# A streaming encoder layer on eight cores: norm row spread by TensorE, last block in halves, order replanned

## The reference

```python
u = rmsnorm(x, norm_mix)
xl, gl, xp, gp, ml, mp = jnp.split(u @ w_in, SPLITS, axis=-1)     # 5632 columns
xc = causal_conv(xl)                                              # depthwise, width 4
r, i = sigmoid(block_diag(xc, w_rg_a) + b_a), sigmoid(block_diag(xc, w_rg_i) + b_i)
a = exp(-8 * r * softplus(-lam))
h = scan(h = a * h + sqrt(1 - a * a) * i * xc)                    # along the frames
A = h * silu(gl)
B = (pooled_means_minus_frame(xp) @ w_pool + b_pool) * pool_scale * silu(gp)
x = x + (sigmoid(ml) * A + sigmoid(mp) * B) @ w_out
x = x + sigmoid(rmsnorm(x, norm_ple) @ w_ple_gate) * (p @ w_ple)
y = rmsnorm(x, final_norm)
```

## Time and profile before

| what | value |
|---|---|
| median of 3 runs (lowest, highest) | 1022.29 us (1022.08, 1022.36) |
| the profiled execution | 1022.78 us |
| its span (slowest core, core 2) | 1020.9 us |
| spans of cores 0 to 7 | 1018.6, 1009.3, 1020.9, 1011.4, 1018.9, 1009.3, 1009.8, 1016.7 us |
| busy: PE, DVE, ACT, POOL | 941.1, 782.4, 758.2, 310.7 us |
| DMA | 184.14 MB, 180 GB/s in the mean |

### The profile page before, as it was taken

One profiled execution on the slowest core, in us unless ns is written; L12 is line 12 of the kernel. 1 busy time (PEld: TensorE's weight loads), 2 busy tenths in 40 slices (PEclk: granted clock), 3 DMA queues, 4 the chain that ended last, 5 costly groups with the idle time before them and its releaser, 6 DMA issues.

```text
span 1020.9 us, 16786 instructions; the slowest of 8 cores (1009.3 to 1020.9 us)
## 1 busy us (share of the span) xinstructions
PE 941.1 (92%) x4545; PEld 435.1 (43%) x4636; DVE 782.4 (77%) x1208; ACT 758.2 (74%) x1275; POOL 310.7 (30%) x576
## 2 busy tenths in 40 slices
PE   3897998499999999999999999999999999999994
PEld 1342443144444444444444444444444445454541
DVE  3755978667697696686969788787969797798864
ACT  3777786766857858769696867778796959999753
POOL 3332424223143142312313123333414243232221
PEclk9998999799999999999999999999999999999998
DMA  8899775898943667466664667465773647467732
GB/s 186 166 251 228 162 169 101 238 229 212 252 117 113 191 200 228 129 198 178 181 188 124 233 164 200 137 199 170 223 200 105 190 135 221 151 188 242 233 99 83
DMA packets 113179, 184.14 MB, mean 180 GB/s; under 512 B 67392, under 2 KB 72000, under 8 KB 113088
## 3 DMA queue, kind: packets, MB, share of 16 engines
q1 hardware_dynamic: 100272, 154.69, 50.8%
q0 software_dynamic: 12816, 28.38, 14.5%
HBM read 155.56 MB, written 29.12 MB: 181 GB/s over the span
## 4 chain that ended last, share of the span: by engine, by line
PE 62%; ACT 14%; issue 9%; DMA 9%; DVE 5%; POOL 0%; ACTq 0%; SPq 0%; DVEq 0%; POOLq 0%
PE psum L814 42%; PE psum L1121 8%; PE psum L1101 8%; DMA wpg<-w_in 4%; PE psum L1128 2%; ACT wk L927 1%; DMA ring<-w_in 1%; ACT L927 1%; DVE wk L868 1%; PE psum L886 1%; DMA xb<-xp 1%; ACT L909 1%; ACT wk L925 1%; ACT u2t L1113 1%; PE psum L889 1%
## 5 line engine op out<-in xcount | busy, mean ns | idle before, releaser
L814 PE MATMUL psum<-ut,ring 128*128 128x512 bf16 x2444 | 555.5, 379 | 9.4 <-ACT wk L1048 2.7
L814 PEld LDWEIGHTS psum<-ut,ring 128*128 128x128 bf16 x2496 | 241.9, 98 | 298.0 <-issue 13.7
L868 DVE SCALAR_TENSOR_TENSOR wk<-xw,cvec,wk 128x512 f32<-128x512 f32 x186 | 133.3, 744 | 15.5 <-ACT wk L859 4.0
L732 POOL TENSOR_SCALAR stat<-stat 128x1 f32<-128x1 f32 x99 | 39.8, 402 | 278.3 <-ACT wk L1140 134.1
L1121 PE MATMUL psum<-wpg,u2t 128*128 128x512 bf16 x517 | 119.1, 379 | 2.0 <-DMA u2t<-ub 1.3
L1101 PE MATMUL psum<-wout,mg 128*128 128x512 bf16 x499 | 116.0, 379 | 2.8 <-ACT ws L1048 0.9
L814 PE MATMUL psum<-ut,wpg 128*128 128x512 bf16 x312 | 77.5, 401 | 21.2 <-ACT wk L1050 12.0
L1121 PEld LDWEIGHTS psum<-wpg,u2t 128*128 128x128 bf16 x528 | 51.4, 98 | 64.1 <-issue 3.1
L1101 PEld LDWEIGHTS psum<-wout,mg 128*128 128x128 bf16 x512 | 49.7, 98 | 61.8 <-issue 3.0
L948 POOL COPY hst<-wk 128x1 f32<-128x1 f32 x43 | 51.6, 1212 | 70.9 <-DVE wk L943 67.0
L879 ACT ACTIVATE xcb<-wk 128x512 bf16<-128x512 f32 x62 | 39.1, 630 | 44.7 <-DVE wk L868 44.3
(11 more groups left out here) (189 smaller groups left out, 1480.4 us busy)
## 6 DMA issues: line engine op xcount, KB each, us to landing
ring<-win_bf SPq DMA_DIRECT2D x154, 512.0 KB, 4.6
xb<-xp SPq DMA_DIRECT2D x64, 512.0 KB, 6.1
yp<-xb SPq DMA_DIRECT2D x32, 512.0 KB, 3.3
ring<-w_in POOLq DMA_DIRECT2D x12, 512.0 KB, 8.2
win_bf<-ring POOLq DMA_DIRECT2D x12, 512.0 KB, 15.7
wpg<-w_in POOLq DMA_DIRECT2D x10, 512.0 KB, 9.1
win_bf<-wpg POOLq DMA_DIRECT2D x10, 512.0 KB, 11.6
xb<-w_ple_gate SPq DMA_DIRECT2D x8, 512.0 KB, 5.5
```

The costliest lines, as they stand in the source:

```text
L814: nd("pe", pe_cost(8, N), [lambda e, kc=kc: e.matmul(b.ap[:, 0:N], lhsT=s.ap.rearrange("p (k n) -> p k n", k=8)[:, kc, o:o + 128], rhs=ut_ ...
L868: nd("dve", dve_cost(N), lambda e, j=j, w=w: e.scalar_tensor_tensor(out=av(), in0=xw()[:, :, 3 - j:W - j], scalar=w, in1=av(), op0=ALU.mul ...
```

## The change

- norm_mix is no longer read spread over 128 partitions by one DMA on SP. Two DMAs of 2 KB on ACT's queue bring it as rows of one partition, two float32 matmuls with a row of ones times 32 spread them into PSUM, and DVE copies them to `gmbc`.
- The small vectors (`cvec`) are loaded first on ACT's queue; what is derived from them (`consts` before, with an Exp and an Ln on ACT) comes at the very start.
- pool_scale and final_norm come from the host spread over 128 rows, so that their loads are plain ones.
- The sums of squares of tiles 0 and 1 write their unused output to a work tile, not to `ub`. Weight block 0 waits for x block 2.
- The slots `xb` are tracked in two halves. In the very last prompt block the squares, the last product and the store go by halves of 512 columns (L1275, L1284, L1287 of the new kernel), with one more POOL addition (L1278). The last block of tile 7 and that of tile 8 are turned by TensorE (L1239) and copied from PSUM (L1242 on ACT or L1244 on DVE).
- Every node has a tag of kind, tile and part, and a table `ORDER` adds a shift to its due time; POOL's computing steps have none. Some of the planner's numbers are others.

The core of the diff; of the table and the tags a line or two stand for all:

```diff
 D = 1024
 IN_COLS = 5632
 NPAIR = IN_COLS // 256
-PRM = dict(window=61003.0, lim=113076.0, lag=10051.0, penw=1.36, slack=78.0, evac=255.0, p2=0, c2=0.55, 
-           a2=0.94, an=0.2, cs=12784.0, wl=30305.0, pes=12.0, late=(), wq='pool', wd=6037.0, pet=2, 
...
-           nu=3, nx=3, ac=3)
+           nr=5, nu=3, nx=3, ac=3)
+
+ORDER = {"a0.0": 1759, "a0.1": 11360, "a0.2": 14842, "a0.3": 16186, "a1.0": -5600, "a1.1": -27034, "a1.2": 21723,
...
-        n.eng, n.cost, n.nom, n.tset = eng, cost, nom, tset
+        n.eng, n.cost, n.tset = eng, cost, tset
         if eng != "pe" and any((r[0] if isinstance(r, tuple) else r).pool == "fb" for r in reads):
-            n.nom = nom = nom - PRM["evac"]
+            nom = nom - PRM["evac"]
+        n.tag = self.tag if eng != "pool" or queue is not None else ""
+        n.nom = nom = nom + ORDER.get(n.tag, 0.0)
...
-                d0 = max(s + 900.0, dma_free)
+                d0 = max(s + 1000.0, dma_free)
                 dma_free = d0 + n.nbytes
-                end = dma_free + 1300.0 + PRM["dl"]
+                end = dma_free + 1700.0
                 lat = 60.0
...
-    d_pool_scale = din("pool_scale", [1024])
+    d_pool_scale = din("pool_scale", [128, 1024])
-    d_final_norm = din("final_norm", [1024])
+    d_final_norm = din("final_norm", [128, 1024])
...
-    mkpool("xb", 6, [128, 1024], F32)
+    mkpool("xb", 6, [128, 1024], F32, nsub=2)
...
+    def xb2(v):
+        return [(v, 0), (v, 1)]
+
...
-        return nd(queue, 560.0 if queue == "pool" else SPC,
+        return nd(queue, {"pool": 560.0, "act": 100.0}.get(queue, SPC),
-                  reads=list(reads), writes=[dst], nom=nom, nbytes=nbytes, queue=queue, soft=soft, nb=nb, gates=gates,
+                  reads=list(reads), writes=xb2(dst) if isinstance(dst, V) and dst.pool == "xb" else [dst],
...
+    load(CV, d_vecs, -99000, 200, queue="act")
+    Z.tag = "cv"
+    nd("dve", 100, lambda e: e.tensor_scalar(out=CV2.ap[:, HBA:HBA + 16], in0=CV.ap[:, BA:BA + 16], scalar1=0.5,
+                                             scalar2=None, op0=ALU.mult), reads=[CV], writes=[CV2], nom=-97000)
...
+    nd("act", 250, lambda e: e.activation(out=CV2.ap[:, HCL:HCL + 8], in_=CV.ap[:, LAM:LAM + 8], func=AF.Exp,
+                                          scale=-1.0), reads=[CV], writes=[CV2], nom=-97000, tset=(LN, EXP))
+    nd("act", 250, lambda e: e.activation(out=CV2.ap[:, HCL:HCL + 8], in_=CV2.ap[:, HCL:HCL + 8], func=AF.Ln, bias=1.0),
+       reads=[CV2], writes=[CV2], nom=-97000, tset=(LN,))
...
+    ones = Z.val("ws")
+    nd("pool", 100, lambda e: e.memset(ones.ap[0:1, :], 32.0), writes=[ones], nom=-99000)
+    for hf in range(2):
+        row, bank = Z.val("wk"), Z.val("fb")
+        nd("act", 100, lambda e, row=row, hf=hf: e.dma_start(out=row.ap[0:1, :], in_=d_norm_mix[hf * 512:(hf + 1) * 512].unsqueeze(0)),
+           writes=[row], nom=-98000, nbytes=30, queue="act")
+        nd("pe", 1800, lambda e, row=row, bank=bank: e.matmul(bank.ap, lhsT=ones.ap[0:1, :], rhs=row.ap[0:1, :],
+                                                              start=True, stop=True),
+           reads=[ones, row], writes=[bank], nom=-96000)
+        nd("dve", dve_cost(512), lambda e, bank=bank, hf=hf: e.tensor_copy(
+            out=GM.ap[:, hf * 512:(hf + 1) * 512], in_=bank.ap), reads=[bank], writes=[GM], nom=-95000)
+
...
-        n = load(dst, x_src(tiles[j // 4], j % 4), -90000 + 2000 * j if j < 4 else -22000 + 1000 * j, 1750, gates=gates)
+        n = load(dst, x_src(tiles[j // 4], j % 4), -90000 + 2000 * j if j < 4 else -22000 + 1000 * j, 1600, gates=gates)
         x_first.append(n)
-        if j == 0:
-            load(GM, d_norm_mix.partition_broadcast(128), -89000, 1750)
-            nd("dve", 650, lambda e: e.tensor_scalar(out=GM.ap, in0=GM.ap, scalar1=32.0, scalar2=None, op0=ALU.mult),
-               reads=[GM], writes=[GM], nom=-89000)
-        if j == 3:
-            load(CV, d_vecs, -83500, 300)
-
-    load(G3, d_final_norm.partition_broadcast(128), 150000, 1750, nb=150000)
+
+    load(G3, d_final_norm, 150000, 1650, nb=150000)
...
+            junk = Z.val("wk") if S["idx"] < 2 else u
             nd("act", act_cost(1024, False, acc=True),
-               lambda e, x=x, st=st, u=u: e.activation(out=u.ap, in_=x.ap, func=AF.Square, accum_out=st.ap[:, 0:1]),
-               reads=[x], writes=[st, u], nom=nom)
+               lambda e, x=x, st=st, junk=junk: e.activation(
+                   out=junk.ap if junk.pool == "ub" else junk.ap.bitcast(BF16), in_=x.ap, func=AF.Square,
+                   accum_out=st.ap[:, 0:1]),
+               reads=xb2(x), writes=[st, junk], nom=nom)
             rstd_ops(st, nom)
...
-                turn(u, lambda j=j: ut_v()[:, :, j * 128:(j + 1) * 128], (UT, j), nom, 1800)
+                turn(u, lambda j=j: ut_v()[:, :, j * 128:(j + 1) * 128], (UT, j), nom, 1300)
...
-                    gates = [x_first[2 * k + 1 if k < 2 else 5] if k in (0, 1, 3) else w_first[k - 1 if k < 4 else k - 2]]
-                n = load(s, d_w_in[m], -25000.0 + 2000 * k if gates and k < 4 else nom - PRM["wl"], 3000, queue="pool", gates=gates)
+                    gates = [x_first[(2, 3, 0, 5)[k]] if k in (0, 1, 3) else w_first[k - 1 if k < 4 else k - 2]]
+                n = load(s, d_w_in[m], -25000.0 + 2000 * k if gates and k < 4 else nom - PRM["wl"], 3200, queue="pool", gates=gates)
...
-                load(s, d_wsc[m], nom - PRM["wl"], 1750, reads=[WSC[m]], soft=PRM["sl"])
+                load(s, d_wsc[m], nom - PRM["wl"], 1650, reads=[WSC[m]], soft=PRM["sl"])
...
-                   reads=[s], writes=[WSC[m]], nom=nom + PRM["wd"], nbytes=1750, queue=PRM["wq"], soft=PRM["sw"], paced=True,
+                   reads=[s], writes=[WSC[m]], nom=nom + PRM["wd"], nbytes=2050, queue=PRM["wq"], soft=PRM["sw"], paced=True,
...
+                    op=ALU.add), reads=[(xr, hf), d[hf]], writes=[(xr, hf)], nom=nom)
             nd("act", act_cost(1024, False), lambda e, xr=xr, u2=u2: e.activation(out=u2.ap, in_=xr.ap, func=AF.Copy),
-               reads=[xr], writes=[u2], nom=nom,
...
-                out=u2t.ap, in_=xr.ap, func=AF.Square, accum_out=st.ap[:, 0:1]), reads=[xr], writes=[st, u2t], nom=nom)
+                out=u2t.ap, in_=xr.ap, func=AF.Square, accum_out=st.ap[:, 0:1]), reads=xb2(xr), writes=[st, u2t], nom=nom)
             rstd_ops(st, nom)
-            turn(u2, lambda u2t=u2t: u2t.ap.rearrange("p (k n) -> p k n", k=8), u2t, nom, 1800)
+            end_ = S["idx"] == 7 and j == 3
+            if S["idx"] >= 7 and j >= nt - 1:
+                tb = Z.val("fb")
+                nd("pe", pe_cost(8, 128), [lambda e, u2=u2, tb=tb, c=c: e.transpose(
+                    out=tb.ap.bitcast(BF16)[:, c * 128:(c + 1) * 128], in_=u2.ap[:, c * 128:(c + 1) * 128],
+                    identity=IDB.ap) for c in range(8)], reads=[u2, IDB], writes=[tb], nom=nom)
+                nd("act", act_cost(1024), lambda e, tb=tb, u2t=u2t: e.activation(
+                    out=u2t.ap, in_=tb.ap.bitcast(BF16), func=AF.Copy), reads=[tb], writes=[u2t], nom=nom,
+                   alt=("dve", dve_cost(1024), lambda e, tb=tb, u2t=u2t: e.tensor_copy(out=u2t.ap, in_=tb.ap.bitcast(BF16))))
+            else:
+              turn(u2, lambda u2t=u2t: u2t.ap.rearrange("p (k n) -> p k n", k=8), u2t, nom, 1300)
+            Z.tag = "ce%d.%d" % (S["idx"], j)
             tg = [Z.val("wk"), Z.val("wk")]
             eb = [Z.val("fb"), Z.val("fb")]
             fk = [Z.val("fb"), Z.val("fb")]
...
+            if end_:
+                st3 = Z.val("stat")
+                for hf, q in enumerate((st2, st3)):
+                    nd("act", act_cost(512, False, acc=True), lambda e, xr=xr, q=q, tg=tg, hf=hf: e.activation(
+                        out=tg[hf].ap, in_=xr.ap[:, hf * 512:(hf + 1) * 512], func=AF.Square, accum_out=q.ap[:, 0:1]),
+                       reads=[(xr, hf)], writes=[q, tg[hf]], nom=nom)
+                nd("pool", 110, lambda e, st2=st2, st3=st3: e.tensor_tensor(
+                    out=st2.ap[:, 0:1], in0=st2.ap[:, 0:1], in1=st3.ap[:, 0:1], op=ALU.add), reads=[st2, st3], writes=[st2],
+                   nom=nom)
+                rstd_ops(st2, nom)
+                for hf in range(2):
+                    h_ = slice(hf * 512, (hf + 1) * 512)
+                    nd("dve", dve_cost(512, ptr=1), lambda e, xr=xr, st2=st2, h_=h_: e.scalar_tensor_tensor(
+                        out=xr.ap[:, h_], in0=xr.ap[:, h_], scalar=st2.ap[:, 1:2], in1=G3.ap[:, h_], op0=ALU.mult,
+                        op1=ALU.mult), reads=[(xr, hf), st2, G3], writes=[(xr, hf)], nom=nom)
+                    nd("sp", SPC, lambda e, xr=xr, dst=y_dst(S, j)[:, h_], h_=h_: e.dma_start(out=dst, in_=xr.ap[:, h_]),
+                       reads=[(xr, hf)], nom=nom, nbytes=800, queue="sp", lane=STP.slot.bufs[1 + j + 4 * hf])
+                continue
...
-    def consts():
```

(5 more changed lines are left out.)

79 lines of the change are left out of this document (53 added, 26 removed), and 61 rows, old and new, of the table ORDER.

## The result

The change made the kernel faster by 34 us: 988.2 us (median of 3 runs, 987.0 to 988.3) for 1022.2, ratio 0.9665, with a 95% interval of 0.9646 to 0.9684. A fourth run took 1169.7 us with cores 0 to 3 at a granted clock of 0.81 to 0.82; executions of either kernel fall into such a slow state at times, and the ratios and times here leave them out. A second set of runs, on the same chip as three of the experiments, gave 988.3, ratio 0.9676 (0.9648 to 0.9703). I had predicted 1002, from 990 to 1014. The sign was right; 14 us of the gain I had not seen, and the time lies just outside the range.

The account below looks back on a forecast made before the run. It took the kernel as bound by PE; start -3.5, ramp 0, stall -13.5, steady part 0 and tail -3.2 sum to -20.2, from 1022.8 to 1002.6, about 1002 against the median, range 990 to 1014.

Parts of the forecast that it names:

- Bound by PE, few places with loss: Whole program: PE busy 941.1 of 1020.9 us on core 2, so savings stand only at few places of idling or low clock.
- The term of the steady part: Behind 205 us: little idle PE time to win, more to lose by long ACT stretches; 0, bounds -5 and +12.
- The stall, -13.5: PE's 12.0 us wait at 188 us: ACT's batch is cut in two, slow matmuls and a DVE wait go; bounds -17 and 0.
- Start, -3.5: Before the first projection: norm_mix as two rows lets x3 land sooner, projection at 17.8 for 21.86; bounds +1.3 to -5.
- The rival that gave the start nothing: Start: ACT waits for the vectors or the weight stream sets the ramp; 1006 to 1007 us, chance 0.12.
- ACT's wait for the vectors: Start: all four squares stand behind the vectors' load, expected near 3.9 us; if 10.6 again, the term is +1.3.
- Late weight block and ramp, 0: Ramp to 120 us: follows the start, and the 5.4 us weight wait with slow matmuls stays; 0, bounds -7 and +3.
- Tail, -3.2: End: 10.6 for 13.0 us behind the last matmul (-2.4), DMA transpose wait gone (-0.8); bounds -4 and +1.
- Rival (a): First waits (5.4 + 1.9) and part of the steady idle (5) go too; 990 us, chance 0.2.
- The stretch of ACT at rows 562 to 570: Steady part: 12.2 us of ACT without a read of PSUM, expected to cost between 0.9 and 12; +1 taken.
- The signs I had named: First projection at 17 to 18.5 us, no long waits near 188, PE over 197 of 200, last matmul 10 to 11 before the end.
- a sign of being wrong: Start: the prediction is wrong if, among other signs, the squares wait for the vectors past 6 us.

Follow-up runs that it names:

- batch_joined_tied: New kernel with ACT's batch at 188 us in one piece again, transfers tied to the new kernel's matmul groups: 993.9 us, ratio 0.9719.
- new_start_old_order: Kernel before with only the new start and plain loads of two constants; order, memory slots, transfer ties and end as before: ratio 0.9999.
- mended_tied: New kernel with start steps reordered on ACT, DVE and POOL, fewer POOL steps at the end, transfers tied as there: 984.8 us, ratio 0.9635.

## Why the prediction was wrong, step by step

- **Bound by PE, few places with loss: the reading that failed.** I wrote that the 800 us behind 205 have "some 20 in small pieces, part of them matmul records that are missing", and then "there is little to win (at most 5)". I had judged by core 2, where 91 records are missing, and by one window of 200 us. Core 1 has every record, and PE idles 15.0 us there in 791; on core 2 too, the waits of the same stretch, listed by what ended them, come to 15. The missing records made little of the idle time. Core 1's waits from 205 to 965 us, before and after (total, times, longest), the first rows:

```profile
PE psum L814 <- ACT wk L1048: 2.7, 3, 1.4
PE psum L889 <- ACT wk L892: 1.5, 2, 1.3
PE psum L814 <- ACT wk L1050: 1.2, 2, 0.7
PE psum L886 <- ACT wk L892: 1.0, 1, 1.0
```

```profile
PE psum L994 <- ACT xcb L985: 1.5, 3, 0.6
PE psum L1259 <- ACT ws L966: 1.5, 1, 1.5
PE psum L1252 <- ACT ws L969: 0.4, 1, 0.4
```

  Before, 17 such rows stand, 13 us in all, 11 of them waits for ACT; after, four rows, 3.7 us. The term of the steady part, 0 with bounds -5 and +12, measured -14 on core 2 (9.0 and 5.0; up to 2 of it may belong to the end edit). This is the step that failed, alone the size of the miss.
- **The stall, -13.5**: the mechanism was right (batch_joined_tied); of the 12.0 I had left 3, and 1.4 stayed. The stage from 125 to 200 us of work gave 16.0 on core 2. Mis-sized by 2.5; I had counted the wait, the slow matmuls (1.9, where 5.40 less 3.61 is 1.8) and one xcb wait of 2.6, and the other xcb waits of the earlier trace rows went too.
- **Start, -3.5**: wrong. The rival that gave the start nothing (0.12) was true. ACT's wait for the vectors was the step that I had named; they came at 6.16 (4.43 to 7.22 by core), not 5, and Exp waited for DVE besides, so squares began at 8.68, not 5.6. The float32 matmul takes 2.04, just above my upper bound of 1.9. And of a start that is 1.5 us sooner (new_start_old_order) 0.5 is left by 75 us of work; the rest goes mostly into waits for weights (core 5, 22 to 110 us: 4.7 for 1.2). The small load was not held up as in SP's queue: it landed in 5.0 us, before in 10.6. With the rule of the Trainium skill (DMA: Bandwidth & Descriptors, Queues, rings and completion order), by which each DMA engine goes round between the queues, the trace agrees, as far as a load that was also issued first can show it. The table load took 1.28 with the next activation right behind it, at 8.27. The 2.66 of the Trainium skill (ScalarE: Activation LUTs, What ACT_TABLE_LOAD costs) is 1283 ns for the load and some 1380 for a drain; this trace shows the first and no time for the second.
- **Late weight block and ramp, 0**: by 75 us of work core 2 was 2.9 us ahead (37.0 to 34.1) and core 1, which had no late block before, 3.6 behind (27.7 to 31.3); the mean of the eight went from 31.3 to 26.7. For the slowest core it is a gain, within my bounds.
- **Tail, -3.2**: 0 to 3 by the runs above, too small to tell. Behind the last matmul it gave 0.8 of the 2.4. POOL's added step took 0.98 and the half store landed no sooner.
- **Rival (a)**, the first waits and the steady idle go too, 990 with 0.2, was the one that came true. Of its two parts the steady idle gave 14 where it had 5, and the first waits gave less than its 7.3 (core 2 gained 5.3 up to 125 us of work, the start included), so that its 990 is partly luck. The stretch of ACT at rows 562 to 570, my ground for +12, stands at 617.0 to 628.0 us on core 2; it is 10.9 long and cost 0: PE's waits from 600 to 640 us are none. There too PE had output products (32 matmuls of L1221 from 615.90).
- **The signs I had named**: no wait over 4 us and a clock of 1.00 in 150 to 200 came true, as did over 197 of 200 in 500 to 700. The first projection (20.85 for 17 to 18.5) and the last matmul (12.2 us before the end, for 10 to 11) did not, and a sign of being wrong appeared: the squares waited for the vectors past 6 us.

## What to carry over

Where the bounding engine is at 92%, sum its waits by releaser over the whole program, on a core whose records are complete, before calling the rest noise: many waits of 0.2 to 1.4 us are one term of 14 us, and another order took nearly all of them away. An edit of the code and a plan belong together: old planner numbers on a changed state came out 10 to 25 us slower than the kernel before, and the new start and end in the old order 4 slower (there some stores had moved too). When parts are swapped for a test, keep the order, the memory slots and the ties of the transfers, or the test measures the plan.

## What the runs showed of the hardware

- A float32 matmul of one partition and 512 columns takes 2.04 us in these rows (two records each), more than five times the 0.38 of a bf16 one. The Trainium skill (FP8 and Floating Point Precision, TensorE Precision Notes) says that true float32 takes four passes through the array; an estimate by it, four times 0.38, is some 1.5, and the row is above it.
- A transfer of 2 KB on ACT's queue, the core's first at 1.07, had landed by 2.84; behind the vectors, issued from 1.49 on, the two halves came at 5.05 and 8.51 on core 2.
- POOL's power step on one column takes 0.57 alone. On the eight cores of the new kernel none took over 0.61 unless a DVE product of two SBUF operands ran beside it; of the 401 that had one beside them 139 took over 0.9. One from mended_tied, at 1.50:

```profile
974.33 1.28 DVE L1370 SCALAR_TENSOR_TENSOR xb<-xb,stat,g3bc 128x1024 f32<-128x1024 f32 x1
974.51 1.50 POOL L1355 TENSOR_TENSOR stat<-stat,negh 128x1 f32<-128x1 f32 x1 [0.80 <-DVE stat L1351]
```
